# Rotary multiplications by cosine and sine on VectorE in one piece with the pass, no longer on GpSimd

## What is computed

```
def apply_rope(x, pos):
    half = ROPE_DIMS // 2
    inv = ROPE_THETA ** (-jnp.arange(half, dtype=jnp.float32) / half)
    ang = pos.astype(jnp.float32)[:, None] * inv[None, :]
    cos, sin = jnp.cos(ang).astype(x.dtype), jnp.sin(ang).astype(x.dtype)
    x1, x2, rest = x[..., :half], x[..., half:ROPE_DIMS], x[..., ROPE_DIMS:]
    return jnp.concatenate([x1 * cos - x2 * sin, x2 * cos + x1 * sin, rest], axis=-1)

q, k, v, mq, gate = split_proj(jnp.einsum('bld,de->ble', x, w_in_a[j]), SPLIT_A)
o_mix = mixer_a(...)                    # layer 0; mixer_b in layer 1; both rotate q and k
o_mem = memory_attention(to_heads(mq, MEM_HEADS), mem, w_mkv[i])
y = jnp.concatenate([o_mix, o_mem], axis=1).transpose(0, 2, 1, 3).reshape(b, L, D_INNER)
y = y * jax.nn.silu(gate)
x = layer_norm(ALPHA * x + jnp.einsum('ble,ed->bld', y, w_out[i]), ln_g[i], ln_b[i])
```

## Time and profile before

| | |
|---|---|
| median of 3 runs | 2403.65 us (2402.94 to 2410.18) |
| profiled execution | 2407.48 us |
| its span, first to last instruction | 2405.7 us |
| PE busy | 2217.9 us, 92% |
| DVE busy | 1542.7 us, 64% |
| ACT busy | 1123.4 us, 47% |
| POOL busy | 688.9 us, 29% |
| mean granted TensorE clock | 0.965 |

### The profile page before, as it was taken

The page is one execution under the profiler, slowest core; times in us unless marked ns, Lnnn a source line. Parts: engine busy times, 40 slices in busy tenths (PEclk is TensorE's granted clock), DMA queues, the critical chain, the costliest instruction groups (busy, mean ns, idle before and its releaser), DMA issues.

```text
span 2405.7 us, 32351 instructions
## 1 busy us (share of the span) xinstructions
PE 2217.9 (92%) x11072; PEld 1834.0 (76%) x11072; DVE 1542.7 (64%) x3265; ACT 1123.4 (47%) x2697; POOL 688.9 (29%) x485
## 2 busy tenths in 40 slices
PE   8999999999979959999998999989989999998996
PEld 8887878778868747777776777767767777787775
DVE  6767666676634677666666757666676666574375
ACT  5454445445522334454554554545545455464232
POOL 2222222220000244344334443433444333200022
PEclk9999999999989979999999999999999999999998
DMA  8211111211254521121211212112112121223553
GB/s 258 75 44 54 44 58 40 71 43 50 69 186 137 174 100 37 35 63 46 71 50 53 63 41 62 50 57 69 35 58 63 45 71 49 80 67 120 179 174 123
DMA packets 206605, 190.35 MB, mean 79 GB/s; under 512 B 19940, under 2 KB 160300, under 8 KB 206444
## 3 DMA queue, kind: packets, MB, share of 16 engines
q1 hardware_dynamic: 206444, 188.29, 25.0%
HBM read 160.01 MB, written 28.23 MB: 78 GB/s over the span
## 4 chain that ended last, share of the span: by engine, by line
PE 49%; issue 16%; POOL 16%; DVE 14%; DMA 3%; ACT 2%; SPq 0%; POOLq 0%; DVEq 0%; ACTq 0%
PE bank L1100 8%; PE bank L1102 8%; PE bank L1101 7%; POOL work L997 7%; PE bank L1150 7%; POOL work L1000 6%; PE bank L1176 5%; PE bank L1270 4%; PE bank L1274 4%; PE bank L1276 4%; PE bank L1164 3%; DVE work L1634 2%; DVE ring L1551 2%; DMA x_ops<-y_scratch 2%; POOL sums L976 1%
## 5 line engine op out<-in xcount | busy, mean ns | idle before, releaser
L1100 PE MATMUL bank<-x_ops,ring 128*128 128x512 f32 (+1 forms) x1808 | 863.4, 478 | 25.6 <-issue 16.8
L1102 PE MATMUL bank<-x_ops,ring 128*128 128x512 f32 (+1 forms) x1808 | 707.0, 391 | 0.0
L1101 PE MATMUL bank<-x_ops,ring 128*128 128x512 f32 (+1 forms) x1808 | 704.0, 389 | 0.0
L1551 DVE TENSOR_TENSOR ring<-raw,ring 128x512 fp32r<-128x512 f32 x400 | 296.3, 743 | 450.5 <-ACT ring L1316 450.0
L997 POOL TENSOR_TENSOR work<-work,trig 32x512 f32<-32x512 f32 (+3 forms) x152 | 216.3, 1428 | 881.3 <-DVE work L1626 730.6
L1100 PEld LDWEIGHTS bank<-x_ops,ring 128*128 128x128 f32 x1808 | 351.1, 194 | 92.2 <-issue 30.7
L1102 PEld LDWEIGHTS bank<-x_ops,ring 128*128 128x128 f32 x1808 | 346.1, 191 | 72.7
L1101 PEld LDWEIGHTS bank<-x_ops,ring 128*128 128x128 f32 x1808 | 352.0, 195 | 63.8 <-issue 19.9
L1150 PE MATMUL bank<-work 128*128 128x256 f32 (+2 forms) x896 | 315.7, 436 | 79.5 <-DVE soft L1658 79.4
L1377 ACT COPY work<-bank 128x256 f32<-128x256 f32 (+2 forms) x448 | 164.4, 367 | 450.2 <-PE bank L1164 449.4
L1316 ACT CAST ring<-raw 128x512 fp32r<-128x512 f32 x400 | 247.9, 622 | 236.7 <-PE bank L1276 205.2
(11 more groups left out here) (88 smaller groups left out, 2741.1 us busy)
## 6 DMA issues: line engine op xcount, KB each, us to landing
raw<-in_w_in_b SPq DMA_DIRECT2D x160, 256.0 KB, 3.0
raw<-in_w_out SPq DMA_DIRECT2D x128, 256.0 KB, 2.8
raw<-in_w_in_a SPq DMA_DIRECT2D x80, 256.0 KB, 3.0
work<-weight_scratch SPq DMA_DIRECT2D x24, 768.0 KB, 5.1
y_scratch<-work SPq DMA_DIRECT2D x32, 512.0 KB, 2.7
x_ops<-y_scratch SPq DMA_DIRECT2D x64, 256.0 KB, 3.5
raw<-in_w_mkv SPq DMA_DIRECT2D x32, 256.0 KB, 4.6
work<-in_x SPq DMA_DIRECT2D x4, 1024.0 KB, 8.2
```

The costliest lines, as they stand in the source:

```text
L1100: nc.tensor.matmul(dst, w_h, x_h, start=start, stop=False, skip_group_check=again)
L1101: nc.tensor.matmul(dst, w_h, x_l, start=False, stop=False, skip_group_check=again)
L1102: return nc.tensor.matmul(dst, w_l, x_h, start=False, stop=stop, skip_group_check=again)
L1551: nc.vector.tensor_tensor(ring[:, n % RING, 1, :], src, ring[:, n % RING, 0, :].bitcast(F32), ALU.subtract).then_inc(w_lo, 1)
```

## The change

`rotate` goes away. Its multiplication by the cosines comes behind the shuffle in `turn`, behind a wait for `rope_turned`; its multiplication by the sines comes at the head of `turn_ends`, and the wait for `rope_mul` in front of the addition is now one of VectorE for itself. The steps at which `turn` and `turn_ends` stand are the same. The second half of memory head 1's output in layer 1 is multiplied by its gate two steps later.

```
-            t1, t0 = ((T0 + 28, T0 + 29), (T0 + 32, T0 + 34), (T0 + 28, T0 + 29),
+            t1, t0 = ((T0 + 28, T0 + 29), (T0 + 32, T0 + 36), (T0 + 28, T0 + 29),
...
-            def rotate(key):
-                g, e, h = key
-                dest = pairs[g].dests[e]
-                pool.wait_ge(rope_turned, rope_no[key] + 1)
-                for view, take in dest.views(h, ROPE):
-                    nc.gpsimd.tensor_tensor(view, view, take(cosb[:, h * HALF:(h + 1) * HALF]),
-                                            ALU.mult)
-                for view, take in turned_views(dest, h):
-                    mul = nc.gpsimd.tensor_tensor(view, view, take(sinb[:, h * HALF:(h + 1) * HALF]),
-                                                  ALU.mult)
-                mul.then_inc(rope_mul, 1)
...
-                    if T in ropes_at[layer]:
-                        rotate(ropes_at[layer][T])
...
                 sh.then_inc(rope_turned, 1)
+                dve.wait_ge(rope_turned, rope_no[key] + 1)
+                for view, take in dest.views(h, ROPE):
+                    nc.vector.tensor_tensor(view, view, take(cosb[:, h * HALF:(h + 1) * HALF]),
+                                            ALU.mult)
 
             def turn_ends(key):
                 g, e, h = key
                 dest = pairs[g].dests[e]
+                for b, take in turned_views(dest, h):
+                    mul = nc.vector.tensor_tensor(b, b, take(sinb[:, h * HALF:(h + 1) * HALF]),
+                                                  ALU.mult)
+                mul.then_inc(rope_mul, 1)
                 dve.wait_ge(rope_mul, rope_no[key] + 1)
                 for (view, _), (b, _) in zip(dest.views(h, ROPE), turned_views(dest, h)):
                     add = nc.vector.tensor_tensor(view, view, b, ALU.add)
```

## The result

The changed kernel takes 2331.12 us at the median (2329.64 to 2333.35, four runs), the kernel before, run beside it on the same chip, 2403.3: a ratio of 0.9696, with a 95% interval of 0.9674 to 0.9718. The forecast was 2336. The profiled execution took 2329.64 us with a span of 2327.8, which is 77.9 us less than the profiled one of before; that one had run 4 us above its median, so the two medians lie only 72 us apart.

The account below looks back on a forecast made before the run. PE, busy 92%, was taken as the bound; gains count only in its waits for VectorE and its clock. Terms 26 + 16 + 3 + 8 + 3 + 9 + 3 = 68 us give 2339.5 profiled, 2336 median; range 2303 to 2384.

Parts of the forecast that it names:

- site A: Layer 1, 11 PE waits of about 3.6 us for the mask fall to 1.1 us: 26 us gained (15 to 37).
- site B: Layer 1, 11 PE waits of 2.9 us for the mask, hardly shorter: 3 us gained (-5 to 11).
- clock: PE's half clock behind stalls: 51 us at site A go, saving 16 us; at site B most stays, 3 us.
- layer 0: Layer 0, 12 PE waits for the normalisation, 9.7 us in all: 9 us gained (0 to 9.7).
- third stall: Layer 1, 6 PE waits of 1.1 to 1.5 us two tiles behind site B: 7.7 us gained (0 to 7.7).
- first head: First head of layer 1, four rotations in its first pair: some 5 us of small stalls, 3 us gained.
- The stretch: VectorE instructions beside GpSimd's rotation run 1.0 to 1.2 us longer; this goes, perhaps 120 us of VectorE's busy time.
- the 0.60 us for each multiplication: What a moved 32x512 multiplication costs VectorE's queue, taken from an addition of the same shape and operands.
- self-wait: A VectorE instruction that waits for VectorE's own last result costs its queue 0.2 us more.
- VectorE's queue is fuller: Rival, chance 0.19: both site A and site B keep stalls over 2 us and their half clock; 2380 us.
- More goes than I count: The second rival, chance 0.08: site A and site B end below 2 us, clock whole; 99 us gained, 2306.
- Slower: Rival, chance 0.06: the stretch isn't GpSimd's rotation, so masks at site B come 3.1 us later; about 2430 us.

Follow-up runs that it names:

- run 4: Not a follow-up run: the words say that the profiled execution of the kernel before "had run 4 us above its median".
- the three `beside` kernels: The changed kernel plus unawaited GpSimd work beside each rotation: two multiplications (ratio 1.0550), one (1.0150), or four memsets (0.9667).
- no_stride: The changed kernel with the order-16 queries reading cosine and sine tables in memory order, not every 16th element: 2328.29 us, ratio 0.9684.
- late: The changed kernel with layer 1's rotations that stood ahead of the masks started and ended 11 to 13 steps later: 2273.06 us, ratio 0.9450.
- late_before: The kernel before, multiplications still on GpSimd, with the same later steps for layer 1's rotations: 2296.65 us, ratio 0.9552.
- beside_write: The changed kernel plus four GpSimd memsets beside each rotation, which read nothing and which nobody waits for: 2327.16 us, ratio 0.9667.
- sine_gpsimd: The changed kernel with the sine multiplication given back to GpSimd and the cosine left on VectorE: 2375.54 us, ratio 0.9882.

## Why the prediction was right, step by step

The direction and the mechanism held, and on the medians the size did: 72 us for a forecast of 68. Part of that is luck. The terms were summed for the profiled execution, where the measured gain is 78, and the execution of before happened to lie 4 us above its median. Of the terms, those of the sites A and B were off by 11 and 9 us in opposite directions and nearly balanced; the clock and layer 0 gave 10 more than forecast. On the span, the terms against what the traces show:

| term | forecast, us | measured, us |
| --- | --- | --- |
| site A, stalls | 26 | 15.3 (39.6 to 11 x 2.21 = 24.3) |
| site B, stalls | 3 | 12.3 (32 to 11 x 1.79 = 19.7) |
| third stall | 8 | 7.7 |
| clock | 16 + 3 | 26 (all that PE's busy time in layer 1 fell) |
| layer 0 | 9 | 12 |
| first head | 3 | 3.1 |
| sum | 68 | 77 of the span's 77.9 |

**The stretch.** Right: 681 ns where the median was 1776, shown by the three `beside` kernels. VectorE's busy time rose by 80 us: the multiplications of 512 columns cost 89.2 + 86.4, the shorter pieces 38 together, so some 133 us of stretch went on balance; I had put 180 and 120. One group went the other way: the split's low part out of `sums`, L1551 before and L1537 after, went from 680 to 761 ns in the mean. Those are 11 of its 180, of 1.9 to 2.1 us, each beside GpSimd's copy in `keys_in_runs` (L997, now 1.96 us), in heads 2 to 12; before, the copy took 2.37 us there and the split 0.67. So the two engines still meet once a head; who is held has changed.

**Site A: the step that was mis-sized.** From the pass to the end of the mask I had 9.2 us (8.2, and 1.0 held by GpSimd); the timeline above gives 1059.79 - 1050.17 = 9.62. The hold was right: L1004 of GpSimd ends at 1051.92, and the cosine that started in its time ends 0.94 us later, at 1052.86. What failed is the 0.60 us for each multiplication, taken from an addition of the same shape and operands: the table is read with a stride just here, 0.35 to 0.4 us more, twice. Self-waits cheaper than I thought (below) take 0.3 us off again. The rest is small: counted from the first pass of the site, the second came 0.3 us later than my 1068.0, with the same stride in its neighbour's rotation (1.06 and 1.02 us), and PE wanted its bank 0.27 us earlier than before. Together that is the 1.1 us between my stall and the 2.21; `no_stride` shows 0.83 us of it to be the stride. Of the other parts no run was made.

**Site B.** I held this queue for full, and it gained 1.1 us for each head and not 0.3. The self-wait is the term that was mis-sized: I priced it at 0.2 us from one pair in the earlier trace rows. After the change (timeline of VectorE at B):

```profile
1078.83 0.69 DVE L1537 TENSOR_TENSOR ring<-raw,ring 128x512 fp32r<-128x512 f32 x1 [0.48 <-ACT ring L1302]
...
1080.64 0.67 DVE L1623 TENSOR_TENSOR work<-work,trig 32x512 f32<-32x512 f32 x1
1081.34 0.68 DVE L1628 TENSOR_TENSOR work<-work 32x512 f32<-32x512 f32 x1
...
1082.15 0.74 DVE L1612 STREAM_SHUFFLE work<-work 32x512 f32<-32x512 f32 x1
...
1094.14 0.27 DVE L1652 CUSTOM_DVE_ANT_0 work<-bank,masks 128x128 f32<-128x128 f32 x1
```

The addition starts 0.70 us behind the sine that it waits for, and an instruction without such a wait 0.60: the self-wait costs 0.10 us. My pair of 0.80 us was an addition and the pass that waits for it; that pair is still 0.81 apart (1081.34 to 1082.15), but the sum had no more of such. A cosine behind its pass starts 0.78 us after it (1082.93), and without a wait it is 0.64 (1069.05 to 1069.69 before), so 0.14. My sum had six self-waits in this stretch, which makes some 0.5 us of the 0.9 by which it missed. From L1537 to the mask it is 15.3 us, for 16.5 before and 15.5 to 16.2 by my sum.

**The clock.** The chain "less stall, whole clock" held in sum, since 105 us at half clock became 41. Its detail did not. I had it that a stall under 1.5 us leaves the clock alone, and A's would all be so short: A's were 2.21, and a fall follows 5 of 11; at B I expected the half clock to stay, and it stayed behind 2 of 11. The premise itself stood: where A's stalls are 1.38 us, in `no_stride`, none is followed by a fall. The price was 0.41 us for one at half clock over the whole layer, where two heads had given 0.32; `no_stride` and `late` read 0.7 to 0.8, so the price is the least certain part of this sum. So 19 us became 26 by two errors that add: more half clock gone, each a little dearer.

**Layer 0 and the rest.** The 12 stalls of 0.88 us went in full: PE's idle time there fell by 9.7 us, and its busy time by 2.5, which I hadn't counted. The gate step cost nothing.

**The rivals.** The upper bounds of the second, 99 us, give 2305 on the median and not 2306, which changes nothing. "VectorE's queue is fuller" was right of site A (stalls above 2 us) but not of B, so its 2380 didn't come. "More goes than I count" was right of B's stalls and of the clock's share. "Slower" was a real mechanism with the wrong sign of its condition: the stretch is GpSimd's.

What the prediction didn't ask is whether the rotation's second half had to lie ahead of the masks at all. `late` and `late_before` answer it with more time than the change itself.

## What to carry to other kernels

When work moves between two engines that hold each other, part of the gain is in the instructions that stay, here some 133 us of VectorE's time beside 140 us of its waits: read the least against the median duration of a line, and count how much of the other engine's reading lies beside it. Price a moved instruction by its own access pattern as well as its shape, since a nearest row with the same shape may read in order where the moved one doesn't. And before paying for a busy queue by changing engines, look whether the work is needed by the time that it is queued: here some twelve steps of delay gave 107 us alone, the other engine 72, and both 130.

## What the runs showed of the hardware

- **A strided fp32 input costs VectorE half as much again.** 32x512 with one operand at every 16th element takes 1.02 to 1.06 us, in order 0.67 to 0.68, where GpSimd reads nothing beside it. The Trainium skill, page "SBUF — State Buffer", section "Door 1: The DMA port swizzle", says that SBUF has 16-byte cachelines, that each access which crosses to a new one pays a penalty, and that fp32 can so stride over 4 elements for free; it gives no size for the penalty. Our stride is 64 bytes, and the rows agree with it in direction.
- **Holding is one of reading, and mutual.** GpSimd's 512 memsets of 947 ns each left VectorE's sum at 681 ns and the kernel no slower; its multiplications cost 112 us (128 of them) and 206 us (256), and themselves took 1.8 to 2.0 us in the mean, 1.4 at the least.
- **A self-wait on VectorE is cheap**: 0.10 us over the spacing of 0.60 between a multiplication and its addition, 0.2 where a shuffle waits for an addition.
- **Equal stalls, unequal clock.** Behind the stall of 1.8 us at site B the granted clock is 0.50 in 2 of 11 heads of the changed kernel, and in 9 of 11 with A's stall shortened; behind the stall of 2.2 us at A in 5 of 11, and in 9 of 11 in `beside_write`. Why isn't settled. Stalls of 1.4 to 1.7 us were followed by it in none of 32 cases, those of 2.6 to 3.0 us in `sine_gpsimd` in all 22.
